# One hybrid DiT block on Trainium2: router by token halves, gate rows through device memory, weight loads between the projection loads

## The reference, cut to what matters

```python
mx = jnp.split((sc @ w_mod[l] + b_mod[l])[:, None, :], 6, axis=-1)   # shifts, scales and gates of 1024
ox, oc = token_mixer(hx, hc, rows, lb, w_in[l], ..., w_proj_a[l], w_proj_b[l], w_out[l], need_ctx)
x = x + mx[2] * ox                                       # 256 tokens x 1024
hx2 = modulate(rmsnorm(x, norm2_g[l]), mx[3], mx[4])     # h * (1 + scale) + shift
x = x + mx[5] * hier_moe(hx2, ...)
return rmsnorm(x, final_g)

def branch_merge(...):
    pa = (ya * jax.nn.gelu(ay)) @ w_proj_a
    pb = (yb * jax.nn.silu(og)) @ w_proj_b
    return (jax.nn.sigmoid(ga) * pa + jax.nn.sigmoid(gb) * pb) @ w_out

def hier_moe(h, w_rg, b_rg, w_re, b_re, w1, w3, w2):     # 4 groups of 8 experts
    p_grp = softmax(t @ w_rg + b_rg); pg, gi = top_k(p_grp, 1)
    pe, ei = top_k(softmax(logits of that group), 2)
    for e in range(32):
        y = y + cw[:, e:e + 1] * ((silu(t @ w1[e]) * (t @ w3[e])) @ w2[e])
```

## Time and profile before

| what | value |
|---|---|
| median of 3 runs | 1012.51 us (1012.46 to 1014.66) |
| profiled execution, its own time | 1014.44 us |
| its span, first to last instruction | 1012.7 us |
| PE busy | 872.0 us, 86% |
| DVE busy | 377.8 us, 37% |
| ACT busy | 315.4 us, 31% |
| DMA | 284.34 MB, mean 281 GB/s |

### The profile page before, as it was taken

The page is one execution under the profiler, slowest core; times in us unless marked ns, Lnnn a source line. Parts: engine busy times, 40 slices in busy tenths (PEclk is TensorE's granted clock), DMA queues, the critical chain, the costliest instruction groups (busy, mean ns, idle before and its releaser), DMA issues.

```text
span 1012.7 us, 13214 instructions
## 1 busy us (share of the span) xinstructions
PE 872.0 (86%) x4798; PEld 541.1 (53%) x4798; DVE 377.8 (37%) x892; ACT 315.4 (31%) x575; POOL 65.3 (6%) x109
## 2 busy tenths in 40 slices
PE   4799999999999999999998999586655746799786
PEld 2568686868686868688856534222121211343421
DVE  2348484848485757573123724100001000011101
ACT  6264646464655555550003301101010010110211
POOL 1011111111111111120000000000000000000000
PEclk9899999999999999999997999988787887899998
DMA  9966363545454454408698699999999999999993
GB/s 346 324 150 183 97 176 104 167 112 161 119 154 126 146 133 139 110 0 270 199 429 348 260 429 422 425 432 426 429 426 428 428 428 427 427 427 430 426 424 145
DMA packets 128384, 284.34 MB, mean 281 GB/s; under 512 B 6433, under 2 KB 100833, under 8 KB 115553
## 3 DMA queue, kind: packets, MB, share of 16 engines
q1 hardware_dynamic: 127728, 283.30, 74.7%
q10 hardware_dynamic: 624, 0.62, 0.2%
HBM read 282.86 MB, written 1.05 MB: 280 GB/s over the span
## 4 chain that ended last, share of the span: by engine, by line
PE 63%; DMA 29%; issue 3%; SPq 2%; DVE 2%; ACT 1%; POOL 1%; DVEq 0%; ACTq 0%; POOLq 0%
PE bank L550 37%; DMA arena<-in_w 26%; PE bank L847 9%; PE bank L856 4%; PE bank L779 3%; DMA arena<-in_w_mod 2%; PE bank L836 2%; PE bank L866 1%; SPq L339 1%; PE bank L583 1%; PE bank L655 1%; PE bank L672 1%; PE bank L681 1%; PE bank L636 1%; PE bank L635 1%
## 5 line engine op out<-in xcount | busy, mean ns | idle before, releaser
L550 PE MATMUL bank<-arena 128*128 128x256 f32 (+3 forms) x1792 | 402.0, 381 | 4.4 <-DVE arena L1276 3.8
L550 PEld LDWEIGHTS bank<-arena 128*128 128x128 f32 x1792 | 299.2, 191 | 88.8 <-issue 59.2
L847 PE MATMUL bank<-arena 128*32 128x512 f32 (+1 forms) x1024 | 155.8, 656 | 69.9 <-DMA arena<-in_w 69.9
L847 PEld LDWEIGHTS bank<-arena 128*32 128x32 f32 (+1 forms) x1024 | 44.4, 126 | 179.4 <-issue 104.5
L856 PE MATMUL bank<-arena 128*32 128x512 f32 (+1 forms) x512 | 81.1, 680 | 29.5 <-DMA arena<-in_w 29.5
L1598 DVE TENSOR_TENSOR arena<-arena,bank 128x512 f32<-128x512 f32 x10 | 10.3, 1030 | 231.3 <-PE bank L847 231.3
L1152 ACT ACTIVATE arena<-bank 128x512 f32<-128x512 f32 x10 | 6.0, 597 | 201.7 <-PE bank L847 201.7
L1605 DVE TENSOR_TENSOR arena<-bank,arena 128x512 f32<-128x512 f32 x20 | 13.8, 691 | 146.9 <-PE bank L856 146.9
L856 PEld LDWEIGHTS bank<-arena 128*32 128x32 f32 (+1 forms) x512 | 22.0, 130 | 81.2 <-issue 49.2
L1156 ACT ACTIVATE arena<-bank 128x256 f32<-128x256 f32 x10 | 3.8, 384 | 141.3 <-PE bank L901 141.3
L836 PE MATMUL bank<-arena 128*128 128x128 f32 x352 | 42.6, 281 | 1.7 <-DVE arena L1578 1.7
(11 more groups left out here) (304 smaller groups left out, 899.0 us busy)
## 6 DMA issues: line engine op xcount, KB each, us to landing
arena<-in_w SPq DMA_DIRECT2D x92, 2048.0 KB, 26.8
arena<-in_w_in SPq DMA_DIRECT2D x72, 512.0 KB, 7.0
arena<-in_w_mod SPq DMA_DIRECT2D x12, 2048.0 KB, 8.4
arena<-in_w SPq DMA_DIRECT2D x8, 1024.0 KB, 25.6
arena<-in_w_proj_a SPq DMA_DIRECT2D x8, 512.0 KB, 3.8
arena<-in_w_proj_b SPq DMA_DIRECT2D x8, 512.0 KB, 5.2
arena<-in_w_out SPq DMA_DIRECT2D x2, 2048.0 KB, 9.5
arena<-in_x SPq DMA_DIRECT2D x4, 512.0 KB, 5.1
```

Of the source, the lines that this page charges most:

```text
L550: i = mm(dst, w(k), rhs(k), start=k == 0, stop=k == KT - 1)
L847: i = mm(acc[w * b:w * b + w, :], xg[:, k, w * b:w * b + w], wtile(kind, b, u)[:, k, :], start=k == 0, stop=k == KT - 1)
```

## The change

1. SP (`fetch`): F0 to F4 are issued between the pairs, one behind each of pairs 2 to 6, and both parts of w_out ahead of pair 2.
2. F10 and F11 are loaded in halves: the first halves wait for the first half of unit 0's w1 matmuls (`m1_half`).
3. `gate_rows`, the diagonals and `spread`/`turned` are gone. PE transposes `modB` once, ACT stores it (16 KiB) to device memory and loads from there gate1, gate2 (512 KiB each, broadcast to all partitions) and `mod_pk`.
4. The router runs per token half: `route(0)` and `ranks(0)` around the last quarter of w_out, half of the first gather ahead of `route(1)`; `idle_work` are matmuls whose result nobody reads. DVE takes a part of the copies `xg` of unit 0 (`xg_first`).
5. The shift's part of the logits is one matmul with the sum `w_sum` instead of eight.

```diff
-            for i in range(2):
-                sp.dma_start(wo[:, 4 * i:4 * i + 4, :], wo_v[:, 4 * i:4 * i + 4, :]).then_inc(S("wo_in"), 16)
-                if i == 0:
-                    for b in range(2):
-                        proj_loads(2 + b, b, False)
-            with sp.Fori(2, KT // 2) as m:
-                for b in range(2):
-                    proj_loads(m, b, False)
...
+                if n == 10:
+                    sp.wait_ge(S("m1_half"), 1)
+                    for i in range(2):
+                        sp.dma_start(wslot(k, i, at_u)[:, 0:2 * D], src[k][experts[i]][:, 0:2 * D]).then_inc(S("in_w2_1"), 16)
                 if n >= len(RING):
                     free(*LOADS[n - len(RING)][:2])
-                sp.dma_start(wslot(k, b, at_u), src[k][experts[b]]).then_inc(S(f"in_{k}_{at_u % 2}"), 16)
+                part = slice(2 * D if n in (10, 11) else 0, SLOT)
+                sp.dma_start(wslot(k, b, at_u)[:, part], src[k][experts[b]][:, part]).then_inc(S(f"in_{k}_{at_u % 2}"), 16)
+
+            for i in range(2):
+                sp.dma_start(wo[:, 4 * i:4 * i + 4, :], wo_v[:, 4 * i:4 * i + 4, :]).then_inc(S("wo_in"), 16)
+            sp.wait_ge(S("gb_mm"), this(HEADS - 1))
+            for m in range(2, KT):
+                proj_loads(m, m % 2, False)
+                if m < 7:
+                    fetch(m - 2)
...
-                if first:
-                    gate_rows(b)
...
+                if first and b == 0:
+                    turn_mod()
...
+                pe.transpose(bank[6][0:4 * KT, 0:P], modB[:], ident[:]).then_inc(S("mod_rows"), 1)
...
+            A(modT, bank[6][0:4 * KT, 0:P], ACT.Copy).then_inc(S("mod_rows"), 1)
+            act.wait_ge(S("mod_rows"), 3)
+            act.dma_start(mod_dram.rearrange("(a p) -> a p", p=P), modT).then_inc(S("mod_rows"), 16)
+            act.wait_ge(S("mod_rows"), 19)
+            act.dma_start(gate1, mod_dram[None, 0:D].to_broadcast([P, D])).then_inc(S("mod_in"), 16)
+            act.dma_start(gate2, mod_dram[None, 3 * D:4 * D].to_broadcast([P, D])).then_inc(S("mod_in"), 16)
+            act.dma_start(mod_pk, mod_dram[D:3 * D].rearrange("(j p k) -> p j k", j=2, k=KT)).then_inc(S("mod_in"), 16)
...
+            w_out_half(1, 1, 0, 2)
             pe.wait_ge(S("rt_prep"), 2)
             pe.wait_ge(S("x1T_out"), 2)
+            logits(0, 0, KT)
+            w_out_half(1, 1, 2, 6)
+            turn_x1(1, 0)
+            w_out_half(1, 1, 6, KT)
...
+            gather_first(0, 0)
+            gather_first(0, 1)
+            idle_work(4)
+            pe.wait_ge(S("sel_out"), 2)
...
+            residual(1, 0)
+            inverse_root(0)
+            route(0)
+            residual(1, 1)
+            ranks(0)
             dve.wait_ge(S("x1_T"), 4)
             cp(x1T[:, 4:8, P:], bank[3][:].rearrange("p (k n) -> p k n", k=4)).then_inc(S("x1T_out2"), 1)
...
+            mean_square(1)
+            inverse_root(1)
+            route(1)
+            ranks(1)
```

More of the change, by code:

```diff
@@ L136, in build @@
         aff1 = sb("aff1", 2, KT)
-        aff2 = sb("aff2", KT)
+        aff2 = modB[:, 16:24]
         ssq = sb("ssq", 4)
@@ L772, in _, with w_out_half @@
             pe.wait_ge(S("wo_in"), 32)
-            pe.wait_ge(S("gate_rows"), 2)
-            def w_out_half(t, hf):
-                for k in range(KT):
+            def w_out_half(t, hf, first=0, end=KT):
+                for k in range(first, end):
                     if (t, hf) == (0, 0) and k >= KT - 2:
@@ new lines, in _, with gather_first @@
+            first_banks = [bank[4], bank[2], bank[7], bank[3]]
+            def gather_first(t, half):
+                for kt in range(4 * half, 4 * half + 4):
+                    i = mm(first_banks[kt // 2][:, P * (kt % 2):P * (kt % 2) + P], xn[:, t, P * kt:P * kt + P],
+                           hot[:, t, :], start=t == 0 and kt % 2 == 0, stop=t == 1, skip_group_check=True)
+                return i
+            pe.wait_ge(S("hot_first"), 1)
+            pe.wait_ge(S("xn_out"), 1)
+            gather_first(0, 0)
@@ L1131, in _ @@
                 A(src_, src_, ACT.Exp).then_inc(S("rt_exp"), 1)
-            act.wait_ge(S("rt_mm"), 2)
-            A(mod_pk.rearrange("p a b -> p (a b)"), bank[6][:, 0:2 * 8], ACT.Copy).then_inc(S("x1T_out"), 1)
-            act.wait_ge(S("x1T_out"), 4)
+            act.wait_ge(S("mod_in"), 48)
+            for half in range(2):
+                act.wait_ge(S("mx"), this(0, half))
+                for k in range(2):
+                    kt = 4 * half + k
+                    i = A(xg[:, kt, :], bank[(4, 7)[half]][:, P * k:P * k + P], ACT.Identity,
+                          scale=mod_pk[:, 1, kt:kt + 1], bias=mod_pk[:, 0, kt:kt + 1])
+                i.then_inc(S("xgc"), 1)
             def xg_out(half, g):
@@ L1144, in xg_out @@
                 i.then_inc(S("xgc"), 1)
-            for half in range(2):
-                xg_out(half, 0)
             def hidden(q, more=True):
@@ new lines, in ranks @@
+            def ranks(t):
+                dve.wait_ge(S("rank_mm"), t + 1)
+                link(stt(rt_w[:, 2, t, :], bank[(7, 5)[t]][:, 0:NE], 1.0, rt[:, 5, t, :], ALU.add, ALU.mult))
+                w = P // 2
+                for e in range(2):
+                    i = stt(hot[:, t, w * e:w * e + w], slot_no[:, 0:w], 1.0,
+                            rt_w[:, 2, t, e:e + 1].to_broadcast([P, w]), ALU.add, ALU.is_equal)
+                i.then_inc(S("hotc" if t else "hot_first"), 1)
+            residual(0, 0)
@@ L1565, in _, with xg_first @@
-            dve.wait_ge(S("sel_out"), 1)
-            dve.wait_ge(S("rank_mm"), 1)
-            link(stt(rt[:, 11], bank[0][:, 0:2 * NE].rearrange("p (t n) -> p t n", t=2), 1.0, rt[:, 8],
-                     ALU.add, ALU.mult))
-            ts(rank, rt[:, 11], 1.0, None, ALU.subtract)
-            link(ts(rk[:, :, 0:FIXED], rt[:, 11, :, 0:FIXED], 1.0, None, ALU.subtract))
+            rt_one, rt_two, rt_rank = rt[:, 3], rt[:, 4], rt_w[:, 2]
+            def xg_first(half):
+                dve.wait_ge(S("mod_in"), 48)
+                dve.wait_ge(S("mx"), this(0, half))
+                for k in range(2):
+                    kt = 4 * half + 2 + k
+                    i = ts(xg[:, kt, :], bank[2 + half][:, P * k:P * k + P], mod_pk[:, 1, kt:kt + 1],
+                           mod_pk[:, 0, kt:kt + 1], ALU.mult, ALU.add)
+                i.then_inc(S("xg_first"), 1)
```

305 lines of the change are left out of this document (146 added, 159 removed).

## The result

| | before | changed |
|---|---|---|
| median | 1013.59 us (1012.46 to 1014.96, 4 runs) | 1028.87 us (1028.64 to 1029.74, 4 runs) |
| ratio | 1 | 1.0153, 95% interval 1.0131 to 1.0175 |
| profiled execution, its span | 1014.44 us, 1012.7 us | 1029.74 us, 1028.0 us |

The change makes the kernel 1.5% slower, 15.3 us by the medians. The forecast was 1021 us, a range of 1012 to 1027 us: right in its sign and too small, and the result lies 1.9 us above the range.

The account below looks back on a forecast made before the run. Expert-weight DMA bounds the kernel from about 570 us, its start set by PE reaching unit 0. Terms 12.9 + 0.6 - 4.0 = 9.5 us, less 0.9 slack, give +8.6 us: 1021 us, range 1012 to 1027.

Parts of the forecast that it names:

- W to E: From issue of w_out part 1 to end of projections: queued prefetch bytes delay the last pair, 12.9 us later.
- E to T: From end of projections to end of w_out, with half the router work inside: costs 0.6 us.
- T to G: From end of w_out to `gated(0)`: per-half router gains 4.0 us, DVE's list decides, PE waits 4.7 us.
- G to F20: From `gated(0)` to issue of the weight load awaiting w2 of unit 1: follows `gated(0)`, no cost of its own.
- slack of the ring: Ten-place expert-weight buffer: the load awaiting w2 of unit 1 had queued 0.9 us, which absorbs that much delay.
- behind the landing of F20: Rest of the weight stream after the load awaiting w2 of unit 1: the end moves with it, nothing added.
- rival 1: Projections: DMA serves pairs and prefetch side by side, so the end comes 7.7 us earlier, 1005 us; chance 0.08.
- rival 2: Projections: pairs take 2.4 us each between large loads, total +0.2 us, 1013 us, no change; chance 0.12.
- The term for the gate rows: Projections: 1.05 MB from ACT over the same DMA engines adds 2.4 us ahead of the last pair.
- rival 3: Before `gated(0)`: DVE is not late, the router stretch gains 8.6 us, total +4.0 us, 1016.5 us; chance 0.12.
- rival 4: Around `gated(0)`: PE's 4.7 us wait lowers its clock, costing 3.4 us, 1024.5 us; chance 0.12.
- the upper bound of the sum: Whole sum: projection-stage bytes at 413 GB/s (2.3 us more) and router's small matmuls at half speed (2 us) give +13.

Follow-up runs that it names:

- e11: The kernel before, unchanged, profiled once more for a second trace: 1014.99 us (one run).
- e1: Kernel before plus only the prefetch between the pairs, with both w_out parts ahead of pair 2: 1024.58 us, ratio 1.0103.
- e2: Changed kernel without the prefetch, SP's old load order restored: 1015.44 us, 1.001 of the kernel before.
- e10: Changed kernel with the order table moved off gm's memory and `gated(0)` after two of four sums: 1023.25 us, 1.0083 of the kernel before.
- e5: Changed kernel with SP's old load order, and gate1, gate2 and mod_pk loaded only after projection 6: 1016.37 us, 1.0013 of the kernel before.
- e3: Changed kernel with the second part of w_out behind pair 3 instead of ahead of pair 2: 1028.12 us, 1.0144 of the kernel before.
- e4: Changed kernel with F10 and F11 loaded whole instead of in halves: 1028.54 us, 1.0151 of the kernel before.
- e6: Changed kernel with SP's old load order and without the five idle matmuls: 1015.95 us, 1.0014 of the kernel before.
- e7: Changed kernel, SP's old load order, order table off gm's memory, `gated(0)` after two of four sums: 1010.06 us, 0.9956 of the kernel before.
- e12: Like e7, but gate2 alone loaded only after projection 6: 1006.45 us, 0.9924 of the kernel before.
- e8: The edits of e5, e6 and e7 together, on SP's old load order: 1009.28 us, 0.9949 of the kernel before.

## Why the prediction came out as it did

| step | forecast | measured |
|---|---|---|
| W to E | +12.9 us | +14.6 us |
| E to T | +0.6 us | +0.7 us |
| T to G | -4.0 us | -3.2 us |
| G to F20 | 0 | +2.4 us |
| slack of the ring | -0.9 us | -0.1 us |
| behind the landing of F20 | 0 | -1.5 us (-0.4 us against e11's trace) |
| sum | +8.6 us | +12.8 us (+14.0 against e11's trace) |

The steps are rounded one by one.

**The mechanism was right.** Bytes ahead of projection 7 set E. e1 showed it by adding the prefetch alone (E +12.0 us), e2 by taking it away (E -0.3 us). Of rival 1, "*The prefetch stays hidden*", and rival 2, "*Pairs run at full rate between large loads*", nothing was seen: five steps from pair 2 to pair 7 took 42.9 us (landings at 479.01 and 521.90 us), 8.6 each, and the forecast was 8.7.

**W to E was 1.7 us too small.** The start of the sum has 2.0 us of it: pair 2 was due 18.7 us after W (2.7 of latency, 9.8 for w_out, 3.8 for the pair, 2.4 for gate rows) and landed after 20.7 us; w_out part 2 took 6.5 us behind part 1 instead of 4.9. The five steps gave 0.6 us back, and the last projection took 7.1 us instead of 6.9. A long wait before projection 2 followed from these terms (pair 2 at 18.7 us, PE ready 11.4 us after W), but the text spoke of 1.8 us before each projection; it was 9.32 us there, nothing before projection 3, 0.45 us before projection 4 and then 1.47 to 1.51 us. The term for the gate rows was good: the changed kernel and e1 differ at E by 2.6 us, the forecast for them was 2.4.

**T to G** came out at 30.5 us against 29.7, with the stall where the forecast put it: PE waited 5.70 us before G (4.7 worked out). e10 confirms that it is DVE: rival 3 is wrong. That the sum hit so well is in part luck. It took the matmuls behind T at the full clock, as the changed kernel's trace has them; the same rows took 33.2 us from T to G in e2 and e5, whose clock fell there, and 31.5 us in e3.

**The step that failed is the one between G and F20, costed at nothing.** It measured +2.4 us, the largest miss of one term. It was rival 4, "*The clock falls in the new gap*", at 3.4 us. The clock did fall: transposes and gather took 1.11 and 5.74 us, 0.66 and 3.74 in e10, together 2.45 us on the path. All traces agree: G to F20 is 42.3 us in the eight traces with a wait of at most 1.5 us ahead of G, 44.7 to 44.8 in the changed kernel, e3 and e4, and 43.8 to 44.0 in e2, e5 and e6, which have that wait and a shorter gather behind it. I had put the fall beside the forecast as another case, at 0.12. It is no other case: the forecast itself said that PE would wait 4 to 5 us there, and the same wait is what rival 4 needs. The 2.4 us are more than the 1.9 us by which the range was missed; but W to E, T to G and the slack together were short by more. The bounds had the same fault: the upper bound of the sum (+13, 1025.5 us) and rival 4 (+3.4) can hold together, and make about 1029 us, while the range ended at 1027. That the measurement is 1028.87 is chance: the terms behind the +13, bytes at 413 GB/s and the router's matmuls at half speed, are not what the trace shows (the clock is 1.00 from T to U).

**The slack of 0.9 us was not there for F20**: it landed 8.36 us after its issue against 8.5 before. The forecast of 7.6 us held for F14 only (7.64).

**The rest is not explained.** By the medians the change costs 15.3 us, by the profiled executions from W 12.8 to 14.0 us. And of the 7.9 us between 1021 and 1028.87, 1.1 us is the kernel before itself: the forecast stood on its median of 1012.51 us, with the result it had 1013.59. What lies behind the landing of F20 differs by 1.2 us between the two traces of the kernel before (386.1 and 384.9 us), and W by 5.5 us over all traces (what it moves with is in the last section). So few profiles cannot divide the remaining 1.3 to 2.5 us; their cause stays open.

**Where the expected gain went.** The change has two gains of its own, 3.4 us of PE at the gate matmuls and 4 us at the router, and e2 shows neither in the total. Of the first, e5 has 1.8 us at E against the kernel before: 0.9 us goes to pair 2, which lands no earlier for it, and the rest is not divided. The gate rows' 1.05 MB beside the first pairs cost another 1.5 us (e2 against e5). The second is there in the changed kernel, 3.2 us from T to G, and in e2 only 0.5, because the clock fell behind T for 6.8 us and U came 2.8 us later; another 1.5 us goes behind G, again with the clock. What e7 recovers is something else: the 5.7 us that DVE is late at `gated(0)` whatever PE has gained, and the clock behind it.

The Trainium skill, "DMA: Bandwidth & Descriptors", section "Specifications", counts rows of 512 B as line rate. By an estimate from that, a pair would take 2.4 us (its 1.05 MB at the 429 GB/s of the earlier trace rows). These runs disagree: behind F0 to F4 the second load of a pair landed 3.2 to 3.6 us after the F load ahead of it, 295 to 330 GB/s. The 277 GB/s that the sum took is nearer.

## What to carry to other kernels

Free time of DMA ahead of a stage is worth something only if the consumer's first load is what waits; count the bytes that a queue has to serve before the load on the path, and give a prefetch only what fits beside PE's pace (here 1 MiB beside each of four projections was free, and 2 MiB beside five cost 12 us). Removed work can uncover a wait: the gate matmuls also covered the wait for pair 2, and with them gone PE waited 0.9 us for it. When a wait is cut short on PE, look at once for the engine that is late next, and ask why its list must come first: here it was two buffers in one place, and parting them was worth 5.4 us, where the rest of the change without the prefetch gave nothing. Where a forecast says itself that PE will stand for some 5 us, the lower clock behind that wait is a term of its sum and no rival.

## What the runs showed of the hardware

- **Waits of PE and the clock.** In waits of 9.32, 5.70 and 5.69 us (projection 2 and G of the changed kernel, G of e2) the granted clock went to 1.2 GHz, for 10.2, 6.8 and 6.8 us. Around waits of 4.13 and 3.65 us (e3) it did so for 6.8 us each, and right behind one of 3.34 us (e1) for 3.4 us. In waits of 0.45 to 1.51 us, four in a row, it stayed at 2.4 GHz. The Trainium skill, "TensorE: Matmul & The Clock Gate", Part 1, has an idle array fall to the lower clock; the traces agree for the long waits.
- **The same instructions, three lengths.** From T to U the changed kernel, e12 and e2 take 11.5, 12.6 and 14.3 us, at a mean clock of 1.00, 0.86 and 0.76. The changed kernel and e2 differ only in SP's order. A single trace over this stretch is good to 3 us.
- **W moves with the clock of the first 50 us.** There the granted clock is at 1.2 GHz for 3.4 us in e8 (W at 454.1 us), 6.8 us in five traces (455.7 to 456.7), 10.2 us in five (457.5 to 458.4) and 13.7 us in three, the changed kernel among them (458.3 to 459.6). Whether that is most of the spread of one kernel's times is not shown: between the two traces of the kernel before W differs by 1.7 us and the time by 0.55 us.
- **Issuing can take long.** With w_out and pair 2 under way, SP's rows show 3.2 to 6.5 us for one issue (9.3 us once in e3), against 0.37 us on an empty queue. Bytes under way are not enough for it: in the kernel before, all 30 issues of F loads between 501.50 and 637.3 us took 0.33 to 0.51 us, with several loads ahead of them. What holds SP is open.
- **A small load behind others waits too.** `mod_pk` (8 KiB) stands behind gate1 and gate2 on ACT's queue. It landed 7.6 us after its issue beside the pairs, and in e5, beside F loads, after 25.9 us (508.02 to 533.88 us), 10.4 us behind gate2. In e12 it stands behind gate1 alone and took 3.8 us.
